# Chunk scores of an HGRN2 mixer turned back by whole transposes, and a samples' product over 128 rows

## What is computed

```python
def step(S, inp):                      # one chunk of HGRN_CHUNK = 16 tokens
    qc, kc, vc, gc = inp
    G = jnp.cumsum(gc, axis=1)
    qg = qc * jnp.exp(G)
    att = jnp.einsum('blhd,bshd->bhls', qg, kc * jnp.exp(-G))
    att = jnp.where(causal, att, 0.0)
    o = jnp.einsum('bhls,bshv->blhv', att, vc) + jnp.einsum('blhd,bhdv->blhv', qg, S)
    g_last = G[:, -1]
    S = S * jnp.exp(g_last)[..., None] + jnp.einsum('bshd,bshv->bhdv', kc * jnp.exp(g_last[:, None] - G), vc)
    return S, o
...
q, f, v, gate = jnp.split(x @ w_in, 4, axis=-1)     # 16 heads of 128
```

## Time and profile before

| | |
|---|---|
| device time, median of 3 executions | 2013.73 us (2012.64 to 2013.85) |
| span of the profiled execution | 2015.7 us |
| busy: TensorE, its weight loads | 1951.5 us (97%), 1763.9 us (88%) |
| busy: VectorE, ScalarE, GpSimd | 1244.4 us (62%), 930.6 us (46%), 1008.8 us (50%) |
| HGRN2 recurrence in the trace | 1062 to 1442 us |

### The profile page before, as it was taken

How to read it: one execution, slowest core, us unless ns; L and a number is a source line. 1 busy time by engine, 2 the same in 40 slices (tenths; PEclk the granted TensorE clock), 3 DMA queues, 4 the chain that set the end, 5 groups by cost and what they waited for, 6 DMA issues and landing times.

```text
span 2015.7 us, 35615 instructions
## 1 busy us (share of the span) xinstructions
PE 1951.5 (97%) x13890; PEld 1763.9 (88%) x13890; DVE 1244.4 (62%) x2220; ACT 930.6 (46%) x1557; POOL 1008.8 (50%) x1249
## 2 busy tenths in 40 slices
PE   7999999999999999999999999999999999999997
PEld 5998989798888988897889999999998889989976
DVE  5988342426887787755147777777454157874552
ACT  3676522334555555342354444443243347674333
POOL 4776704026555655250356666566631337776602
PEclk8999999999999999999999999999999999999998
DMA  4444476535444544487353444444586344445870
GB/s 130 149 147 135 135 250 231 208 105 174 124 116 132 151 132 140 138 297 241 113 170 108 130 130 130 137 136 146 165 313 211 132 148 141 135 148 166 292 231 27
DMA packets 332615, 324.64 MB, mean 161 GB/s; under 512 B 19768, under 2 KB 313056, under 8 KB 332448
## 3 DMA queue, kind: packets, MB, share of 16 engines
q1 hardware_dynamic: 330944, 321.49, 49.8%
q10 hardware_dynamic: 1504, 0.87, 0.2%
HBM read 292.16 MB, written 29.61 MB: 160 GB/s over the span
## 4 chain that ended last, share of the span: by engine, by line
PE 75%; DVE 14%; ACT 5%; issue 2%; DMA 2%; POOL 1%; SPq 1%; DVEq 0%; ACTq 0%
PE ps L773 10%; PE ps L774 10%; PE ps L778 10%; PE ps L1458 5%; PE ps L1467 4%; PE ps L1261 3%; PE ps L1524 2%; PE ps L888 2%; PE ps L763 2%; PE ps L765 2%; PE ps L764 2%; ACT wh L1713 2%; DVE work L2543 2%; PE ps L1602 1%; PE ps L1541 1%
## 5 line engine op out<-in xcount | busy, mean ns | idle before, releaser
L1693 POOL TENSOR_TENSOR wl<-raw,wh 128x256 fp32r<-128x256 f32 x1216 | 1003.3, 860 | 979.1 <-ACT wh L1713 978.9
L1713 ACT ACTIVATE wh<-raw 128x1024 fp32r<-128x1024 f32 x304 | 311.8, 1053 | 202.1 <-PE ps L778 49.8
L773 PE MATMUL ps<-Hh,wh 128*128 128x320 f32 x1200 | 372.2, 324 | 2.8 <-DVE work L2563 0.9
L774 PE MATMUL ps<-Hl,wh 128*128 128x320 f32 x1200 | 360.4, 314 | 0.0
L773 PEld LDWEIGHTS ps<-Hh,wh 128*128 128x128 f32 x1200 | 230.0, 192 | 11.3 <-DVE work L2427 2.3
L774 PEld LDWEIGHTS ps<-Hl,wh 128*128 128x128 f32 x1200 | 230.4, 192 | 2.1
L2258 DVE TENSOR_SCALAR work<-ps 128x512 f32<-128x512 f32 (+8 forms) x220 | 100.3, 474 | 170.9 <-PE ps L871 39.8
L778 PE MATMUL ps<-Hh,wl 128*128 128x320 f32 x1200 | 201.1, 310 | 0.0
L778 PEld LDWEIGHTS ps<-Hh,wl 128*128 128x128 f32 x1200 | 183.2, 189 | 0.1
L773 PE MATMUL ps<-Oh,wh 128*128 128x320 f32 x512 | 152.2, 310 | 3.7 <-DVE Ol L3004 3.7
L774 PE MATMUL ps<-Ol,wh 128*128 128x320 f32 x512 | 151.1, 308 | 0.0
(11 more groups left out here) (439 smaller groups left out, 3922.0 us busy)
## 6 DMA issues: line engine op xcount, KB each, us to landing
raw<-rg_w_in SPq DMA_DIRECT2D x128, 256.0 KB, 3.5
raw<-hg_w_in SPq DMA_DIRECT2D x128, 256.0 KB, 4.8
raw<-ssd_w_in SPq DMA_DIRECT2D x96, 256.0 KB, 3.9
work<-cache_mem_k SPq DMA_DIRECT2D x40, 512.0 KB, 6.3
work<-cache_mem_v SPq DMA_DIRECT2D x40, 512.0 KB, 5.1
raw<-rg_w_out SPq DMA_DIRECT2D x64, 256.0 KB, 3.6
raw<-x_w_k SPq DMA_DIRECT2D x64, 256.0 KB, 3.6
raw<-x_w_v SPq DMA_DIRECT2D x64, 256.0 KB, 3.7
```

Of the source, the lines that this page charges most:

```text
L773: pe.matmul(ps[:, bank, 0:n], high(half, k), mh[:, k, 0:n], start=(k == 0), stop=False)
L774: pe.matmul(ps[:, bank, 0:n], high(half, k), ml[:, k, 0:n], start=False, stop=False)
L1693: ins = pool.tensor_tensor(out, src, wh[:, parted(n) % HALVES, r:r + 2].bitcast(F32), ALU.subtract)
L1713: act.activation(wh[:, nx.n % HALVES], raw[:, slot, :, half * P:(half + 1) * P], ACT.Copy).then_inc(hi_ready, 1)
```

## The change

The scores are turned back by four whole transposes of 128 x 128 instead of four products with a selection of 64 columns of the identity. The result then fills the 512 columns of bank 4, and VectorE picks each chunk's 16 columns out of every 32 when it masks. Since bank 4 is full, the samples' scores and the last state's product go to bank 5, the first state's product to bank 6. This changes which buffers must be free before what: T&S(j, 1) takes two waits ahead of its first transpose that stood behind its last, and turn_back waits for the readers of bank 6. The samples' product L1332 takes all 128 rows of `hg_v` and `hg_att` instead of 64, with zeros in the added rows of `hg_att`, set once at the start.

```diff
@@ turn_and_score, TensorE
                     if h == 1:
                         pe.wait_ge(*past("hg_kt_read", i * 2 + 1))
                         pe.wait_ge(*past("hg_s1_read", i * 2 + 1))
+                        pe.wait_ge(*past("hg_att_ready", i * 2 + 1))
+                        pe.wait_ge(*past("hg_sf_read", i * 2 + 1))
...
                     pe.transpose(ps[0:64, 5, 256:384], hg_k[:, h, SEQ:NT], ident[:]).then_inc(S("hg_kt_full"), 1)
-                    if h == 1:
-                        pe.wait_ge(*past("hg_att_ready", i * 2 + 1))
-                        pe.wait_ge(*past("hg_sf_read", i * 2 + 1))
@@ turn_back, TensorE
                     pe.wait_ge(*past("hg_kt_read", n))
-                    pe.matmul(ps[:, 5, 384:512], hg_kt[:, 0, :], hg_v[:, 0, hv], start=True, stop=True).then_inc(S("hg_s1_full"), 1)
+                    if n > 1:
+                        pe.wait_ge(*past("hg_o_read", n - 1))
+                        pe.wait_ge(*past("hg_osq_ready", n - 1))
+                    pe.matmul(ps[:, 6, 384:512], hg_kt[:, 0, :], hg_v[:, 0, hv], start=True, stop=True).then_inc(S("hg_s1_full"), 1)
                     pe.wait_ge(*past("hg_raw_read", n))
-                    own = ident[:].rearrange("p (g r) -> p g r", g=4)[:, :, 0:16]
                     for T in range(2):
                         for low in range(2):
-                            at = T * P + 64 * (1 - low)
-                            pe.matmul(ps[:, 4, at:at + 64], hg_sq[:, T, P * low:P * low + P], own, start=True, stop=True)
-                    pe.matmul(ps[0:64, 4, 256:320], hg_ks[:, h, :], hg_q[i % 2][:, h, SEQ:NT], start=True, stop=True).then_inc(S("hg_att_full"), 1)
+                            at = 256 * T + P * (1 - low)
+                            pe.transpose(ps[:, 4, at:at + P], hg_sq[:, T, P * low:P * low + P], ident[:])
+                    pe.matmul(ps[0:64, 5, 0:64], hg_ks[:, h, :], hg_q[i % 2][:, h, SEQ:NT], start=True, stop=True).then_inc(S("hg_att_full"), 1)
@@ last_state, TensorE (VectorE's and ScalarE's readers of banks 4 and 5 follow the new places)
-                    pe.matmul(ps[:, 4, 384:512], hg_kt[:, 1, :], hg_v[:, 1, hv], start=True, stop=True).then_inc(S("hg_s2_full"), 1)
+                    pe.matmul(ps[:, 5, 128:256], hg_kt[:, 1, :], hg_v[:, 1, hv], start=True, stop=True).then_inc(S("hg_s2_full"), 1)
@@ outputs, TensorE
-                    pe.matmul(o(2 * P, NT), hg_v[0:64, 2, hv], hg_att[h][0:64, 2 * P:NT], start=True, stop=False, skip_group_check=True)
+                    pe.matmul(o(2 * P, NT), hg_v[:, 2, hv], hg_att[h][:, 2 * P:NT], start=True, stop=False, skip_group_check=True)
@@ scored, VectorE
-                    did(tt(hg_att[h][:, 0:SEQ].rearrange("p (t c) -> p t c", t=2), ps[:, 4, 0:SEQ].rearrange("p (t c) -> p t c", t=2),
-                           upper[:].unsqueeze(1).broadcast_to([P, 2, P]), MUL))
-                    tt(hg_att[h][0:64, SEQ:NT], ps[0:64, 4, SEQ:NT], s_causal[0:64], MUL).then_inc(S("hg_att_ready"), 1)
+                    by_chunk = lambda v: v.rearrange("p (t g c) -> p t g c", t=2, g=8)
+                    did(tt(by_chunk(hg_att[h][:, 0:SEQ]), by_chunk(ps[:, 4, :])[:, :, :, 0:16],
+                           upper[:].rearrange("p (g c) -> p g c", g=8).unsqueeze(1).broadcast_to([P, 2, 8, 16]), MUL))
+                    tt(hg_att[h][0:64, SEQ:NT], ps[0:64, 5, 0:64], s_causal[0:64], MUL).then_inc(S("hg_att_ready"), 1)
@@ VectorE, once, before the first group's keys
+                        for att in hg_att:
+                            did(dve.memset(att[64:P, SEQ:NT], 0.0))
```

More of the change, by code:

```diff
@@ L2036, in s1_copy @@
                     act.wait_ge(*past("hg_s1_full", i * 2 + (h + 1)))
-                    act.activation(hg_s1[h], ps[:, 5, 384:512], ACT.Copy).then_inc(S("hg_s1_read"), 1)
+                    act.activation(hg_s1[h], ps[:, 6, 384:512], ACT.Copy).then_inc(S("hg_s1_read"), 1)
                 def square_out(i, h):
@@ L2754, in last_state @@
                         wait("hg_stored", i * 48)
-                    stt(hg_sf[:, h, :], hg_s1[h], hg_eA[i % 2][:, 2 * h + 1, 8:9], ps[:, 4, 384:512], MUL, ADD).then_inc(S("hg_sf_read"), 1)
+                    stt(hg_sf[:, h, :], hg_s1[h], hg_eA[i % 2][:, 2 * h + 1, 8:9], ps[:, 5, 128:256], MUL, ADD).then_inc(S("hg_sf_read"), 1)
                 def gated(i, h):
```

## The result

The changed kernel takes 2001.74 us (median of four executions, 1998.19 to 2004.64) against 2013.79 us for the kernel before in the same comparison. The ratio on record is 0.9927 with a 95% interval of 0.991 to 0.9944: 0.73% or 14.7 us faster. The two medians alone lie 12.1 us apart, a ratio of 0.994, inside that interval. Even all the work that I had counted off TensorE, 11.5 us, is less than what came by either reckoning, though the upper end of the interval, 11.3 us, leaves room for it.

A forecast was written before the change was run, and what follows sets the result against it. TensorE, busy in 97% of the span, was taken as the bound, with the v weights' loop nearly equal in the recurrence. 0.72 + 2.16 + 1.1 + 4.3 = 8.3 us off 2013.7 gave 2005.4 us, range 2001 to 2011.

The forecast's parts named there:

- The selection products: L1302 in 16 turn_backs: four transposes take 0.67 us instead of 1.04, saving 0.37 each, 5.9 us in all.
- the samples' product: L1332 in 16 outputs: at 128 rows two steps take 0.44 us instead of 0.79, saving 0.35 each, 5.6 in all.
- The moved waits: T&S(j, 1) and turn_back wait for more buffers earlier: cost nothing; at most 0.47 us exposed each time.
- the mask: VectorE's L2745, now reading 16 of every 32 columns: no change from 425 ns; at worst 0.42 us more.
- The sum: Heads outside the six intervals from take_v(1, 0) to take_v(7, 0) give 0.72 + 2.16, the intervals 1.1 + 4.3: 8.3 us.
- the weights' loop: new_state, store, load, v weights, rounding, remainders: 20.8 us beside TensorE's loop; ends three of six intervals, each gaining only 0.37.
- My sign for this: Mean granted clock from 1062 us to the recurrence's end should stay near 0.96.
- The first: Rival: the weights' loop ends every interval, each giving 0.37 only; 2008.6 us, or 2012.5 with three more half-rate stretches; chance 0.25.
- The second: Rival: all 11.5 us come off, and shorter sparse outputs could spare one or two half-rate stretches; 2001 us, chance 0.15.
- The last, slower by the clock: Rival: transposes in turn_back count as idle, 16 half-rate stretches at 1.3 us cost 21; 2026 us, chance 0.06.

The follow-up runs named there:

- 128 rows alone: Kernel before with only the samples' product L1332 over 128 rows instead of 64; ratio 0.9952, median 2007.66 us.
- transposes alone: Changed kernel with the samples' product put back to 64 rows; ratio 0.994, median 2004.61 us.
- before, v weights first: Kernel before with the v weights' loads issued ahead of the second store and load of the samples' states; ratio 0.9969, median 2011.05 us.
- 128 rows alone, v first: Kernel before with the v weights' loads ahead of the samples' second store and load, and L1332 over 128 rows; ratio 0.9872, median 1994.7 us.
- transposes alone, v first: Changed kernel with the v weights' loads ahead of the samples' second store and load, samples' product back at 64 rows; ratio 0.99, median 1998.33 us.
- changed, v first: Changed kernel with the v weights' loads issued ahead of the second store and load of the samples' states; ratio 0.9866, median 1989.5 us.

## Why the prediction was wrong

The granted clock in the table is that of whole executions, least to most; the columns behind it are of the profiled one.

| kernel | ratio to before | granted clock | six intervals, us | half-rate stretches in the recurrence | PE's waits for the v weights, us |
|---|---|---|---|---|---|
| before | 1 | 0.981 to 0.99 | 285.1 | 9 | 4.6 |
| changed | 0.9927 | 0.99 to 0.994 | 271.4 | 2 | 6.5 |
| 128 rows alone | 0.9952 | 0.989 to 0.993 | 279.9 | 4, one of double length | 6.2 |
| transposes alone | 0.994 | 0.985 to 0.992 | 275.3 | 7 | 1.8 |
| before, v weights first | 0.9969 | 0.983 to 0.988 | 279.3 | 9 | 0 |
| 128 rows alone, v first | 0.9872 | 0.991 to 0.994 | 266.2 | 0 | 0 |
| transposes alone, v first | 0.99 | 0.989 to 0.99 | 270.0 | 4 | 0 |
| changed, v first | 0.9866 | 0.991 to 0.993 | 261.4 | 0 | 0 |

- *The selection products, 0.37 us; the samples' product, 0.35 us per head.* Right: 0.40 and 0.35 in the trace, 0.73 together in the clean intervals. Both prices came from rows of the same instruction next to a change of tile.
- *The moved waits cost nothing, the mask costs nothing.* Right: L2747 is at 425 ns, and no wait stands ahead of T&S. Another wait did grow, of gain for VectorE's L2771, 3.4 us in three places, at one of them behind a square on ScalarE that stood behind a rounding. I had not looked at that queue. It isn't the moved waits' doing: with the 128 rows alone it is 4.5 us.
- *The sum, first failed step: "Where the weights' loop ends the interval, only what lies on that loop comes off, turn_back(j, 1) with 0.37".* The loop was not a fixed length. In the three intervals that it ended, my sum leaves 47.3, 47.4 and 46.8 us, 141.5 together; the trace has 45.8, 45.0 and 44.5, 135.3. Of the 6.2 us between, three landings shorter by 1.9 us make 5.7. The rows of the kernel before held the sign of it: from new_state to the last remainder its six passes took 18.0 to 20.8 us, and I had read the longest. The landing isn't all that varies either, for with landings of 3.2 us throughout the changed kernel's passes still took 18.4 to 20.0 us; why is not shown.
- *Second failed step: the clock stood in the sum with nothing.* I had priced a half-rate stretch (1.3 us; it is 1.5), counted nine, and seen that the shorter sparse part "could spare one or two". It spared seven, five of them within the six intervals. In the three intervals that TensorE ended my sum leaves 45.0, 46.6 and 46.5, the trace has 44.0, 45.5 and 46.6, 2.0 us less: most of what the clock gave back went into waits for the weights. Over the six intervals the account closes: 12 heads at 0.73 us are 8.8, five stretches at 1.5 are 7.5, and 2.3 us more of waits take some of it back, 14.0 against the 13.7 measured. My sign for this, a mean clock that stays near 0.96, is missed too: it is 0.99 from 1062 to 1428 us.
- *The rivals.* The first named the right bound, the weights' loop in every interval, and the wrong time for it, since it took the slow store everywhere: it is slow nowhere. The second had the right direction of the clock. The last, slower by the clock, is wrong by sign: half rate became rarer, with the transposes alone too (7 and 4 against 9 and 9, and by the granted clocks in the table). The Trainium skill's sentence on transposes and the full clock ("TensorE: Matmul & The Clock Gate", Part 4: PE-mode transpose) is not borne out by any run here.
- *What each edit is worth* depends on the other bound. With the loop in place 0.48% and 0.60% stand beside 0.73% for both, with 95% intervals that overlap. With the v weights first, the 128 rows take 0.97 points of ratio off (0.9969 to 0.9872), the transposes 0.69, both 1.03: most of the samples' product's gain is the clock, not its 0.35 us.

## What to carry to other kernels

Where the granted clock is below 1.00 in a stage, look at what TensorE did just ahead of each half-rate stretch: making a sparse run of small matmuls cheaper may give back several times its own time (0.35 us in each of 16 heads came with 0.97% here, 19.5 us). Where two loops are nearly equal, price the other loop from its shortest pass in the trace and not from its longest, and ask what in it, such as a landing, differs from one pass to the next. And take the second loop away by itself: one moved block of loads took the changed kernel from 0.9927 to 0.9866, 0.61 points beside the 0.73 of the change under study, and the kernel before only from 1 to 0.9969.

## What the runs showed of the hardware

- A float32 product of 64 rows between products of 128 rows cost 0.79 us for two steps that take 0.44 to 0.45 us at full height, for the same columns. Rows of zeros are cheaper than a change of tile height.
- A half-rate stretch cost 1.5 us of projections. In the kernel before with the v weights first, outputs with a 64-row product were followed by nine in 16 heads; with that product over 128 rows, 0.35 us shorter, by none. TensorE had hardly a wait in either. In the kernel with the 128 rows alone three began within 0.7 us of the end of a wait of TensorE of 2.1 or 3.3 us, and one within such a wait.
- Thirty-two float32 products of 8 columns in a row, with no idle between them, brought on 13.7 us at half rate, beginning 3.1 us behind the start of the first; without them the granted clock is 1.00 there (1000 to 1052 us of the kernel before).
- In 96 stores of 128 KB, each late landing (4.6 to 5.2 us instead of 3.2; 22 of them) had a 16 KB packet of the instruction queue that began 1.7 to 3.2 us behind the issue; 16 others had one and landed within 3.7 us. 128 TensorE instructions more ahead of the layer moved the packets from about 3.1 us behind the issue to 2.5 us ahead of it, in four of six intervals.
